# Attention with key pages as 64 rows of 4 KB in alternate lanes, sample queries and keys loaded by head in the projection, and 16 page places filled ahead

## The chip, the cores and the metric

The kernel runs on one core of a Trainium2 chip. The metric is the device time of one execution in microseconds, as the median of several runs; lower is better. Engines are called TensorE (PE in the profile; PEld is its weight load), VectorE (DVE), ScalarE (ACT), GpSimd (POOL) and SyncE (SP). SyncE issues nearly all DMAs here, in one order.

## The reference, cut to what matters

One step of a decoder layer: a prompt of 1024 new tokens, and 8 sequences with 8 new tokens each and 2048 cached ones in pages of 128. Everything is float32. Each of the two head groups has 512 columns of queries, keys and values.

```python
qd, kd, vd, qs, ks_, vs = project(rms_norm(x), w_in)          # 4 heads of 2*64, 8 heads of 64
past_d = cache_kv_diff[page_table]; past_s = cache_kv_sb[page_table]      # samples only
# group A: differential attention with a bias by distance
s = einsum('bqhcd,bkhcd->bchqk', q, k) * 64**-0.5 + bias      # c: two halves of 64
p = softmax(where(k_pos <= q_pos, s, -inf)); w = p[:, 0] - lam * p[:, 1]
o = rms_norm(einsum('bhqk,bkhe->bqhe', w, v)) * subln_g * (1 - lam_init)
# group B: stick-breaking attention, strictly causal
z = einsum('bqhd,bkhd->bhqk', q, k) * 64**-0.5
a = exp(log_sigmoid(z) + suffix_sum(log_sigmoid(-z)))         # 0 where k_pos >= q_pos
o = einsum('bhqk,bkhd->bqhd', a, v)
x = x + concat(oA, oB) @ w_out;  x = x + hmoe(rms_norm(x));  y = rms_norm(x)
```

The outputs are y and the new keys and values, for prompt and samples.

## The kernel before

**Stages.** `project`, `attention` of the differential kind, `attention` of the stick-breaking kind, `mix_out` (output projection), `route` and `experts` follow one another. Each stage is a block: an engine enters the next one when all engines have ended theirs.

**Projection.** Six groups of columns (keys, queries, values of each kind) by nine tiles of tokens, the ninth being the 64 sample tokens. Keys, and the queries of the sample tile, are turned by TensorE into `kT_ps`, copied by `keep_turned` (L391) and stored by SyncE's `store_turned` (L242) into `scratch_kT` and `scratch_qT`. In the last group SyncE also issues the first 14 places of cache pages (`AHEAD_PAGES`, L690), two places before each step; they lie where the first weight buffers were.

**Pages.** A page of keys is stored in memory turned, as 128 rows (two heads of 64) by four blocks of 128 keys, and a page of values as 128 tokens by 512 columns: 128 rows of 2 KB each. `load_page` (L920) fills one of 20 places with the pages of a pair of sequences, 256 KB each. In attention SyncE follows the order of TensorE's steps; after each step that used a place it waits for that step and issues the pages that come next into that place. A place holds both sequences side by side.

**Attention.** Four turns for each kind. A turn handles one block of two prompt heads (scores, softmax or stick-breaking, output) and one pair of sequences of the samples. The order of steps on each engine is written out by hand, one letter a step (`ORDERS`, L764). The sample's steps in one turn:
- `spread` (L1396) writes the pair's queries into `q_by_block`, which is zero elsewhere, so that one product gives the scores of two heads. In the first differential turn it first copies the loaded `sample_qT` into `sample_q_by_head`, in sixteen copies.
- `page_scores` (L1232): for two pages, eight products of 128x32 weights with 128x256 keys. 32 lanes of the result hold two blocks of one sequence; the 128 lanes are ordered by sequence, head, query.
- `peak`, `weigh` and `share` make the weights, `turn` turns them page by page, and one engine copies eight pages of `turns_and_scores_ps` to `sample_weights_T` (ScalarE L1607 for even groups, VectorE L1472 for odd ones).
- `apply` (L1273) multiplies four slices of 32 weight columns with the page's values into `sample_o_ps`, page after page.
- `rows` (L1475): in the differential kind three one-column operations (sum, inverse, factor), then the scaled copy `sample_o_rows`; `heads` (L1294) brings each head's part out with eight small products.

**The start of an attention stage.** In the differential kind SyncE waits for the projection's stores, then issues `sample_qT` (L1138), the first head's queries, keys, bias and values (L1093 to L1101), the places 14 to 19, `new_keys_T` (L1142) and the new values. At the end of a stage SyncE's last steps are the stores of head outputs (L1132) and loads of new values (L936).

## Time and profile before

| | before |
|---|---|
| Median of 3 runs | 1252.16 us (1251.69 to 1252.54) |
| The profiled execution | 1254.4 us, span 1252.6 us |
| Busy: TensorE, VectorE, ScalarE, GpSimd | 92%, 58%, 47%, 11% |
| DMA | 306.37 MB in 155135 packets, mean 245 GB/s |
| Projection, attention, output projection on, about | 0 to 323, 323 to 750, 750 to the end (us) |

Times are microseconds from the start of the span of one profiled execution. Busy times of an engine are summed over its instructions; matmuls are pipelined, so a busy TensorE isn't TensorE at its peak. The DMA share is the mean busy share of 16 DMA engines; overlapping packets let it go somewhat over 1. A granted clock of 1.00 is the full TensorE clock. "Issue" as the end of a wait is time in which the engine waited for nothing that the profile shows.

### The profile page before, as it was taken

How to read it: one execution, taken by the hardware profiler on the slowest of the kernel's cores; microseconds unless marked ns; L12 is line 12 of the kernel's file. 1: busy time of each engine (PE TensorE's matmuls, PEld its weight loads, DVE VectorE, ACT ScalarE, POOL GpSimd, SP SyncE). 2: the span in 40 equal slices, each digit the busy share in tenths (PEclk: the TensorE clock that was granted, in tenths of full speed). 3: DMA queues.
4: the chain of work that ended last, by engine and by line, in shares of the span. 5: the costliest groups of instructions: out<-in, count | busy, mean ns of one | idle time of the engine just before them, and what ended most of it. 6: DMA issues, size and time to landing. Idle time of an engine off the chain costs nothing. (4 is left out here: it accounts for less than half of the span.)

```text
span 1252.6 us, 23126 instructions
## 1 busy us (share of the span) xinstructions
PE 1146.3 (92%) x7593; PEld 797.8 (64%) x7593; DVE 723.5 (58%) x1078; ACT 591.9 (47%) x1015; POOL 138.8 (11%) x163
## 2 busy tenths in 40 slices
PE   7999999999689999969999999997599999999992
PEld 5877788778345555534655567875366666677771
DVE  6732112220367776568898977453566666666664
ACT  6520212101276776637568554232265555566644
POOL 0100000000011111100000000000123223333311
PEclk9999999999799999979999999999699999999997
DMA  7532424218699899999999935442689999764476
GB/s 265 197 107 70 141 97 127 75 53 277 216 380 382 305 382 380 377 374 381 386 380 382 364 113 187 155 147 103 250 312 365 370 373 302 212 182 102 103 218 193
DMA packets 155135, 306.37 MB, mean 245 GB/s; under 512 B 24359, under 2 KB 49354, under 8 KB 150922
## 3 DMA queue, kind: packets, MB, share of 16 engines
q1 hardware_dynamic: 144762, 271.33, 59.8%
q0 software_dynamic: 9216, 33.56, 11.2%
q8 instruction: 63, 1.03, 0.3%
q14 instruction: 54, 0.44, 0.1%
q10 hardware_dynamic: 1040, 0.00, 0.0%
HBM read 308.31 MB, written 53.67 MB: 289 GB/s over the span
## 5 line engine op out<-in xcount | busy, mean ns | idle before, releaser
L339 PE MATMUL proj_ps<-w_in_split,x_T_hi 128*128 128x512 f32 x608 | 188.9, 399 | 9.2 <-DVE w_in_split L387 9.2
L2566 DVE TENSOR_TENSOR w_gate_up_split<-w_gate_up,w_gate_up_split 128x2048 fp32r<-128x2048 f32 x62 | 139.3, 2288 | 84.3 <-ACT w_gate_up_split L2624 84.3
L2517 PE MATMUL gate_up_ps<-w_gate_up_split,slot_rows_T 128*128 128x512 f32 x744 | 177.7, 394 | 3.2 <-DVE slot_rows_T L2574 3.2
L2517 PEld LDWEIGHTS gate_up_ps<-w_gate_up_split,slot_rows_T 128*128 128x128 f32 x744 | 137.3, 188 | 32.2 <-DVE slot_rows_T L2574 4.4
L339 PEld LDWEIGHTS proj_ps<-w_in_split,x_T_hi 128*128 128x128 f32 x608 | 114.7, 189 | 36.7 <-issue 9.2
L503 ACT ACTIVATE proj_rows<-proj_ps,mean_squares 128x512 f32<-128x512 f32 x32 | 22.0, 688 | 213.6 <-PE proj_ps L339 188.6
L2624 ACT ACTIVATE w_gate_up_split<-w_gate_up 128x2048 fp32r x62 | 115.3, 1912 | 4.9 <-DMA w_gate_up<-in_w_up 3.1
L2539 PE MATMUL expert_out_ps<-w_down,expert_act_T 128*128 x256 | 115.3, 593 | 0.9 <-ACT expert_act_T L2647 0.9
L1192 PE MATMUL turns_and_scores_ps<-head_kT,head_qT 64*128 64x512 f32 (+3 forms) x384 | 86.5, 541 | 20.2 <-DMA head_kT<-scratch_kT 11.2
L339 PE MATMUL proj_ps<-w_in_split,x_T_lo 128*128 128x512 f32 x256 | 101.7, 397 | 0.0
L1786 PE MATMUL mix_out_ps<-w_out_split,oT_split 128*128 128x512 f32 x420 | 101.2, 396 | 0.3 <-DVE w_out_split L1925 0.3
L1786 PEld LDWEIGHTS mix_out_ps<-w_out_split,oT_split 128*128 128x128 f32 x420 | 77.6, 188 | 18.9 <-DVE w_out_split L1925 1.8
L1367 DVE TENSOR_TENSOR_SCAN rest_products<-rest_products 128x128 f32<-128x128 f32 (+7 forms) x64 | 84.3, 1344 | 3.4 <-ACT rest_products L1528 3.4
L333 PE MATMUL proj_ps<-x_T_hi,w_in_split 128*128 128x512 f32 x256 | 83.7, 402 | 0.0
L1556 ACT ACTIVATE weights_T<-turns_and_scores_ps 128x1024 f32<-128x1024 f32 (+6 forms) x80 | 58.9, 742 | 42.6 <-PE turns_and_scores_ps L1206 42.2
L2539 PEld LDWEIGHTS expert_out_ps<-w_down,expert_act_T 128*128 128x128 f32 x256 | 46.2, 190 | 47.1 <-issue 47.1
L2473 POOL DMA_INDIRECT scratch_x<-expert_out,slot_out x32 | 54.8, 1712 | 176.5 <-ACT expert_out L2655 82.3
L1290 PE MATMUL sample_o_ps<-pages,sample_weights_T 128*32 128x256 f32 x1024 | 71.1, 385 | 0.4 <-ACT sample_weights_T L1607 0.4
L1256 PE MATMUL turns_and_scores_ps<-pages,q_by_block 128*32 128x256 f32 x912 | 62.9, 400 | 5.1 <-ACT betas L1532 3.4
L387 DVE SCALAR_TENSOR_TENSOR w_in_split<-w_in_now,g_mix_T,w_in_split 128x512 fp32r<-128x512 f32 x48 | 35.6, 747 | 45.3 <-ACT w_in_split L491 45.3
L1192 PEld LDWEIGHTS turns_and_scores_ps<-head_kT,head_qT 64*128 64x128 f32 x384 | 30.8, 191 | 47.8 <-issue 26.4
L333 PEld LDWEIGHTS proj_ps<-x_T_hi,w_in_split 128*128 128x128 f32 x256 | 48.1, 188 | 14.4 <-DVE qk_transposed L421 2.7
(260 smaller groups left out, 1740.9 us busy)
## 6 DMA issues: line engine op xcount, KB each, us to landing
w_gate_up<-in_w_gate SPq DMA_DIRECT2D x34, 1024.0 KB, 8.5
w_gate_up<-in_w_up SPq DMA_DIRECT2D x34, 1024.0 KB, 10.4
w_down<-in_w_down SPq DMA_DIRECT2D x34, 1024.0 KB, 12.5
pages<-in_cache_v_d SPq DMA_DIRECT2D x128, 256.0 KB, 5.5
pages<-in_cache_kT_s SPq DMA_DIRECT2D x128, 256.0 KB, 5.4
pages<-in_cache_v_s SPq DMA_DIRECT2D x128, 256.0 KB, 5.8
pages<-in_cache_kT_d SPq DMA_DIRECT2D x100, 256.0 KB, 5.9
w_in_now<-in_w_in SPq DMA_DIRECT2D x48, 256.0 KB, 3.6
```

The source lines that it names most:

```text
L333: last = pe.matmul(pj_ps[:, n % PJ_BANKS, 0:c1 - c0], w[g % 2][:, k, at], h[:, k, c0:c1], start=(k == 0 and m == 0), stop=(k == KC - 1 and ...
L339: last = pe.matmul(pj_ps[:, n % PJ_BANKS, :], h[:, k, at], w[g % 2][:, k, :], start=(k == 0 and m == 0), stop=(k == KC - 1 and m == len(pa ...
L1192: last = pe.matmul(ring[places["score", it, i, g]][:, u, 0:k1 - k0], qT[half(u), it % 2, i * P:(i + 1) * P], kT[half(u), it % 2, k0:k1], s ...
L1256: last = pe.matmul(out, q_block[:, e, b, :], keys, start=(part == 0), stop=(part == 1))
L1290: last = pe.matmul(sO_ps[rows, :], sT[0:n, s, rows], page_v[0:n, c // 2, b:b + 2, :], start=(s == 0), stop=(s == D_PAGES - 1))
L1367: dve.tensor_tensor_scan(x, x, x, 1.0, ALU.mult, ALU.bypass).then_inc(scans.sem, 1)
L1556: act.activation(wT[:, at:at + m, :], blocks_of("out", it, i, n)[:, 0:m, :], ACT.Copy)\
L1786: last = pe.matmul(y_ps[:, m % Y_BANKS, :], oT_split[:, n % 2, a, k, :], w_split[:, b, k, c * BANK:(c + 1) * BANK], start=(m > 0 and at == ...
L2517: last = pe.matmul(gu_ps[:, u, :], xT[:, u, a, k, :], gu_split[:, u, b, k, :], start=(k == 0 and m == 0), stop=(k == KC - 1 and m == 2))
L2539: last = pe.matmul(y_ps[:, c, :], aT[:, u, k, :], w_dn[:, bass.ds(at, 1), k, c * BANK:(c + 1) * BANK] .rearrange("p a n -> p (a n)"), star ...
L2566: dve.tensor_tensor(gu_split[:, u, 1, at, :].rearrange("p k (c n) -> p k c n", c=2), raw[:, at, :, :], gu_split[:, u, 0, at, :].bitcast(F3 ...
L2624: act.activation(gu_split[:, u, 0, at, :].rearrange("p k (c n) -> p k c n", c=2), raw[:, at, :, :], ACT.Copy).then_inc(gu_hi.sem, 1)
```

## The change

1. The key cache is handed over with each page as 64 rows (the position in a head) by 8 heads by 128 keys: rows of 4 KB. `load_page` writes the keys of sequence e of a pair into lanes e, e+2, e+4, ... Value pages stay.
2. `q_by_head` holds a pair's queries head by head: lane 2d+e, columns 16u+8e to 16u+8e+7 of head h = 2c+u, zero elsewhere. The four times two products of `page_scores` take the same columns, and the lanes of the result are ordered by head, sequence, query.
3. Where the order by sequence is wanted again (`apply`), the evacuation of the turned weights permutes the columns, in two operations, one per sequence. The factors of the differential rows are computed in `weigh` and brought into that order by one product with a permuted identity (`rows_by_pair`) at the last `apply`.
4. The sample's turned keys and queries are stored by pair member (`scratch_sample_kT`, `scratch_sample_qT`) and loaded by head into alternate lanes in the projection's SyncE order (`load_by_head`, 16 DMAs). The loads of `sample_qT` and `new_keys_T` at the start of attention go, and the sixteen copies and a memset.
5. `AHEAD_PAGES` is 16 instead of 14. VectorE's differential order is edited: the second and third `weigh` of a turn (ww) stand behind its second `turn` (u).

```diff
@@ project
+        by_head_after = {(2, 3): (0, "k"), (3, 3): (0, "q"), (4, 3): (1, "k"), (5, 2): (1, "q")}
@@ store_turned
+                    if tile == PT:
+                        sp.dma_start((t.sample_kT if role == "k" else t.sample_qT_rows)[:, kind * 4:kind * 4 + 4, :, :],
+                                     qkT[:, n % 3, 0:4 * N_SAMPLE].rearrange("p (b e n) -> p b e n", b=4, e=PAIR))\
+                          .then_inc(qkT_stored[n % 3], 16)
+                        return
...
+                def load_by_head(kind, role):
+                    stored = staged[[s for s in turned if s[1] == PT and GROUPS[s[0]] == (kind, role)][0]]
+                    sp.wait_ge(qkT_stored[stored % 3], 16 * (stored // 3) + 16)
+                    src, dst = (t.sample_kT, t.new_kT) if role == "k" else (t.sample_qT_rows, t.sample_qT)
+                    for e in range(PAIR):
+                        for u in range(2):
+                            sp.dma_start(dst[e::PAIR, kind * KIND_HEADS + u:(kind + 1) * KIND_HEADS:2, :, :]
+                                         .rearrange("p b i n -> p b (i n)"),
+                                         src[HEAD * u:HEAD * u + HEAD, kind * KIND_BLOCKS:(kind + 1) * KIND_BLOCKS, e, :])\
+                              .then_inc(by_head_loaded, 16)
...
                     for n, step in enumerate(of_group[g]):
+                        if (g, n) in by_head_after:
+                            load_by_head(*by_head_after[g, n])
...
-        dve.memset(self.t.q_heads[:, :, :, :, :], 0.0).then_inc(self.zeroed, 1)
-AHEAD_PAGES = 14
+AHEAD_PAGES = 16
@@ load_page
-        sp.dma_start(t.page_rows[:, place, e, :, :], src[bass.ds(page, 1), :, :].rearrange("a k n -> (a k) n"))\
-          .then_inc(t.page_loaded[place], 16)
+        if name == "keys":
+            dst = t.page_rows[e::PAIR, place, :, :, :].rearrange("p e b n -> p (e b n)")
+        else:
+            dst = t.page_rows[:, place, e, :, :].rearrange("p b n -> p (b n)")
+        sp.dma_start(dst, src[bass.ds(page, 1), :, :].rearrange("a k n -> (a k) n")).then_inc(t.page_loaded[place], 16)
@@ attention, SyncE
-                    sp.dma_start(q_in[:, :, :], t.qT[:, :, SEQ:SEQ + N_SAMPLE]).then_inc(q_in_loaded, 16)
                     load_head(0)
...
-                    sp.dma_start(t.new_kT[:, :, :], t.kT[:, :, SEQ:SEQ + N_SAMPLE]).then_inc(t.new_kT_loaded, 16)
@@ attention, TensorE: page_scores and apply
                         for c in range(P // COL_TILE):
-                            e, b = c // 2, 2 * (c % 2) + part
+                            h, rows = 2 * c + part, slice(COL_TILE * c, COL_TILE * (c + 1))
...
-                                keys = pages[:, :, e, b, :]
-                            last = pe.matmul(out, q_block[:, e, b, :], keys, start=(part == 0), stop=(part == 1))
+                                keys = pages[:, :, h, :]
+                            last = pe.matmul(out, q_block[:, h, :], keys, start=(part == 0), stop=(part == 1))
...
+                    if kind == DIFF and s == D_PAGES - 1:
+                        pe.wait_ge(zeroed, 1 + PAIR)
+                        pe.wait_ge(sinv.sem, sinv.after(it, 2))
+                        last = pe.matmul(sO_ps[:, 2 * P:2 * P + 1], pair_first[:, :], sstat[:, 3:4], start=True, stop=True)
@@ attention, VectorE: spread, weigh, turn, rows
-                    for odd in range(2):
-                        dve.tensor_copy(q_block[:, :, odd::2, 16 * odd:16 * odd + 16],
-                                        t.q_heads[:, it * PAIR:(it + 1) * PAIR,
-                                                  KIND_BLOCKS * kind + odd:KIND_BLOCKS * (kind + 1):2, :, :]
-                                        .rearrange("p s b u q -> p s b (u q)")).then_inc(q_spread.sem, 1)
+                    for e in range(PAIR):
+                        for u in range(2):
+                            col = 2 * DEC_SEQ * u + DEC_SEQ * e
+                            dve.tensor_scalar_mul(q_block[:, u::2, col:col + DEC_SEQ],
+                                            t.sample_qT[:, KIND_HEADS * kind + u:KIND_HEADS * (kind + 1):2, it, :], t.pair_map[:, e:e + 1])\
+                               .then_inc(q_spread.sem, 1)
...
+                    elif n == 2:
+                        dve.wait_ge(sweighed.sem, sweighed.after(it, 1))
+                        dve.wait_ge(applied.sem, applied.after(it, -1))
+                        dve.tensor_tensor(sstat[:, 5:6], sstat[:, 1:2], sstat[:, 4:5], ALU.add).then_inc(sinv.sem, 1)
...
+                        dve.tensor_tensor(sstat[:, 3:4], sstat[:, 2:3], t.row_factor[:, :], ALU.mult)\
+                           .then_inc(sinv.sem, 1)
...
-                        dve.tensor_copy(sT[:, pages[0]:pages[-1] + 1, :], blocks_of("turn", it, g)[:, 0:len(pages), :])\
-                           .then_inc(read("turn", it, g), 1)
+                        cols = blocks_of("turn", it, g)[:, 0:len(pages), :]
+                        dve.tensor_copy(by_pair(sT[:, pages[0]:pages[-1] + 1, :], 0), of_pair(cols, 0))
+                        dve.tensor_copy(by_pair(sT[:, pages[0]:pages[-1] + 1, :], 1), of_pair(cols, 1)).then_inc(read("turn", it, g), 1)
...
-                        dve.tensor_scalar_mul(o_rows_s[:, :], sO_ps[:, :], sstat[:, 3:4]).then_inc(rows_kept.sem, 1)
+                        dve.tensor_copy(sstat[:, 6:7], sO_ps[:, 2 * P:2 * P + 1]).then_inc(sinv.sem, 1)
+                        dve.wait_ge(sinv.sem, sinv.after(it, 3))
+                        dve.tensor_scalar_mul(o_rows_s[:, :], sO_ps[:, 0:2 * P], sstat[:, 6:7]).then_inc(rows_kept.sem, 1)
@@ attention, ScalarE: turn
+                        act.activation(by_pair(sT[0:n, pages[0]:pages[-1] + 1, :], 0), of_pair(cols, 0), ACT.Copy)
+                        act.activation(by_pair(sT[0:n, pages[0]:pages[-1] + 1, :], 1), of_pair(cols, 1), ACT.Copy)\
+                           .then_inc(read("turn", it, g), 1)
@@ host
-        cache = cache.reshape(n_pool, PAGE, 2, KIND_BLOCKS, P)
-        host["cache_kT_" + name] = cache[:, :, 0].transpose(0, 3, 2, 1).reshape(n_pool, P, HALF_W)
+        cache = cache.reshape(n_pool, PAGE, 2, KIND_HEADS, HEAD)
+        host["cache_kT_" + name] = cache[:, :, 0].transpose(0, 3, 2, 1).reshape(n_pool, HEAD, KIND_HEADS * PAGE)
```

The lane map of `halves` follows the new lane order, and `spread` of the near bias takes its head from the new order too.

## Rows read from the trace of the kernel before

**Rows 1.** Stretches: start:end length, busy us (instructions) per engine, granted clock, DMA share, GB/s

```profile
200.00:300.00 100.00, 100.00 (x442) 80.18 (x441) 20.97 (x31) 12.63 (x21) 0.00 (x0) 1.00 0.36 120
440.00:535.00 95.00, 88.04 (x941) 53.15 (x933) 61.61 (x138) 61.34 (x145) 12.53 (x29) 1.00 1.04 380
535.00:720.00 185.00, 167.86 (x1924) 99.77 (x1926) 158.02 (x213) 115.82 (x204) 0.00 (x0) 0.95 1.04 378
```

**Rows 2.** Waits of TensorE from 331 to 751 us: total us, times, longest

```profile
PE turns_and_scores_ps L1192 <- DMA head_kT<-scratch_kT: 11.2, 1, 11.2
PE turns_and_scores_ps L1192 <- issue: 5.3, 1, 5.3
```

**Rows 3.** SyncE's queue in order of time: start, us, operation, count

```profile
497.83 17.20 SPq L927 DMA_DIRECT2D pages<-in_cache_v_d  x22
...
522.09 12.47 SPq L927 DMA_DIRECT2D pages<-in_cache_kT_s  x18
534.98 0.80 SPq L1132 DMA_DIRECT2D scratch_oT<-head_oT  x2
535.97 1.99 SPq L936 DMA_DIRECT2D new_values<-out_new_kvs  x2
```

**Rows 4.** Order of time around the end of the differential stage, with idle time before

```profile
529.64 1.50 PE L1290 MATMUL sample_o_ps<-pages,sample_weights_T 128*32 128x256 f32 x24
...
533.07 0.60 DVE L1393 TENSOR_SCALAR head_oT<-turns_and_scores_ps,sub_g 128x128 f32<-128x128 f32 x2
...
533.21 1.08 PE L1299 MATMUL sample_o_ps<-ident,sample_o_rows 128*128 128x32 f32 x8 [1.19 <-DVE sample_o_rows L1488]
...
539.63 1.66 PE L1192 MATMUL turns_and_scores_ps<-head_kT,head_qT 64*128 64x128 f32 x8 [5.35 <-issue]
```

**Rows 5.** DMA, 378 to 390 us: packets by size; queue: packets, MB, share

```profile
DMA packets 2541, 4.63 MB, mean 386 GB/s; under 512 B 280, under 2 KB 280, under 8 KB 2541
...
q1 hardware_dynamic: 2541, 4.63, 104.8%
```

**Rows 6.** DMA from 731 to 736 us

```profile
DMA packets 436, 1.55 MB, mean 311 GB/s; under 512 B 57, under 2 KB 57, under 8 KB 436
...
q1 hardware_dynamic: 436, 1.55, 78.3%
```

**Rows 7.** DMA issues from 440 to 535 us: count, KB each, median us to landing

```profile
pages<-in_cache_kT_d SPq DMA_DIRECT2D x32, 256.0 KB, 5.4
pages<-in_cache_kT_s SPq DMA_DIRECT2D x26, 256.0 KB, 5.1
```

**Rows 8.** Stretches of lower clock, columns as in rows 1

```profile
323.50:337.20 13.70, 5.66 (x42) 2.25 (x42) 4.96 (x26) 1.15 (x5) 0.00 (x0) 0.50 0.88 290
535.20:548.80 13.60, 7.56 (x62) 3.65 (x62) 5.71 (x18) 3.72 (x9) 0.00 (x0) 0.50 0.97 357
```

**Rows 9.** SyncE's queue at the start of attention

```profile
324.35 0.61 SPq L1138 DMA_DIRECT2D sample_qT<-scratch_qT  x1
```

**Rows 10.** TensorE's first scores

```profile
331.54 0.80 PE L1192 MATMUL turns_and_scores_ps<-head_kT,head_qT 64*128 64x128 f32 x4 [11.22 <-DMA head_kT<-scratch_kT]
```

**Rows 11.** SyncE's waits from 0 to 320 us

```profile
SPq L239 <- ACT proj_rows L503: 79.4, 25, 5.2
```

**Rows 12.** Operations that are split (min/median/max ns), one of 128x512 (busy, mean ns)

```profile
L1607 ACT ACTIVATE sample_weights_T<-turns_and_scores_ps x16: 250/634/1047, 359.2 to 724.0; 128x1024 f32<-128x1024 f32 x8, 8x128 f32<-8x128 f32 x8
L1472 DVE COPY sample_weights_T<-turns_and_scores_ps x8: 1202/1218/1225, 381.8 to 723.0; 128x1024 f32<-128x1024 f32 x8
...
L1412 DVE COPY q_by_block<-sample_q_by_head x16: 171/189/197, 329.5 to 657.7; 128x64 f32<-128x64 f32 x16
...
L1336 DVE TENSOR_TENSOR scores<-turns_and_scores_ps,near_bias 128x512 f32<-128x512 f32 x24 | 16.5, 686 | 13.0 <-PE turns_and_scores_ps L1192 6.8 <-ACT scores L1521 5.9 <-issue 0.3
```

**Rows 13.** DMA from 321 to 324.3 us: the store of 64 lanes

```profile
DMA packets 80, 0.13 MB, mean 40 GB/s; under 512 B 16, under 2 KB 16, under 8 KB 80
...
q1 hardware_dynamic: 80, 0.13, 17.2%
```

More of the change, by code:

```diff
@@ L555, in keep @@
         return ctx.enter_context(nc.sbuf_tensor(name, shape, dt))
-    t.q_heads = keep("sample_q_by_head", [P, DEC_BATCH, BLOCKS, 2, DEC_SEQ])
+    t.sample_qT = keep("sample_q_by_head", [P, 2 * KIND_HEADS, TURNS, DEC_SEQ])
+    t.new_kT = keep("new_keys_by_head", [P, 2 * KIND_HEADS, TURNS, DEC_SEQ])
     t.near_dec = keep("near_bias_sample", [P, 2, PAGE + DEC_SEQ])
@@ L561, in table_places @@
     t.sub_g = keep("sub_g", [P, 1])
+    t.pair_map = keep("map_of_pair", [P, PAIR])
     t.pages = keep("page_ids", [1, DEC_BATCH * N_PAGES], I32)
@@ L614, in spread @@
             rows = slice(DEC_SEQ * n, DEC_SEQ * (n + 1))
-            for kind, head in ((DIFF, n // 2 % H_DIFF), (STICK, H_DIFF)):
+            for kind, head in ((DIFF, n // PAIR // 2), (STICK, H_DIFF)):
                 sp.dma_start(t.near_dec[rows, kind, :], distances(t, head, DEC_SEQ, PAGE + DEC_SEQ))\
@@ L683 @@
 KIND_BLOCKS = BLOCKS // 2
+KIND_HEADS = 2 * KIND_BLOCKS
 COL_TILE = 32
@@ L1046, in attention @@
         sT_done = count("sample_weights_T_in_psum", V_GROUPS)
-        q_in = sb("sample_qT", [P, BLOCKS, N_SAMPLE if kind == DIFF else 1])
-        q_in_loaded = sem("sample_qT_loaded")
         zeroed = sem("constants_written")
-        q_spread = count("q_by_block_done", 2)
+        q_spread = count("q_by_head_done", 2 * PAIR)
         ps_done = count("page_scores_in_psum", S_GROUPS)
@@ L1054, in attention @@
             speaks = count("sample_peaks_done", S_GROUPS)
-            sinv = count("sample_inverse_sums", 3)
+            sinv = count("sample_inverse_sums", 4)
         else:
@@ L1234, in page_scores @@
                     if g == 0:
-                        pe.wait_ge(q_spread.sem, q_spread.after(it, 1))
+                        pe.wait_ge(q_spread.sem, q_spread.after(it, 2 * PAIR - 1))
                     new = not pages_of_step(kind, ("page_scores", it, g))
-                    if new:
-                        pe.wait_ge(t.new_kT_loaded, 16)
-                    else:
-                        pages = pages_here(pe, "page_scores", it, g)
+                    if not new:
+                        pages = pages_here(pe, "page_scores", it, g).rearrange("p a e b n -> p a (e b) n")
                     place_free(pe, "page_scores", it, g)
@@ L1397, in spread @@
                     if it == 0:
-                        dve.memset(q_block[:, :, :, :], 0.0).then_inc(zeroed, 1)
+                        dve.memset(q_block[:, :, :], 0.0).then_inc(zeroed, 1)
                         if kind == DIFF:
-                            dve.wait_ge(q_in_loaded, 16)
-                            for u in range(2):
-                                for s in range(DEC_BATCH):
-                                    dve.tensor_copy(t.q_heads[half(u), s, :, u, :], q_in[half(u), :, DEC_SEQ * s:DEC_SEQ * (s + 1)])\
-                                       .then_inc(zeroed, 1)
-                            dve.wait_ge(zeroed, 1 + 2 * DEC_BATCH)
+                            for e in range(PAIR):
+                                dve.tensor_copy(by_pair(pair_first[:, :].unsqueeze(1), e), of_pair(t.ident[:, :].unsqueeze(1), e))\
+                                   .then_inc(zeroed, 1)
+                            dve.wait_ge(zeroed, 1 + PAIR)
                         else:
@@ L1410, in spread @@
                     dve.wait_ge(ps_done.sem, ps_done.after(it, -1))
-                    for odd in range(2):
-                        dve.tensor_copy(q_block[:, :, odd::2, 16 * odd:16 * odd + 16],
-                                        t.q_heads[:, it * PAIR:(it + 1) * PAIR,
-                                                  KIND_BLOCKS * kind + odd:KIND_BLOCKS * (kind + 1):2, :, :]
-                                        .rearrange("p s b u q -> p s b (u q)")).then_inc(q_spread.sem, 1)
+                    for e in range(PAIR):
+                        for u in range(2):
[3 more added lines that the diff above has]
+                               .then_inc(q_spread.sem, 1)
                 def page_scores(it, g):
@@ L1606, in turn @@
                         act.wait_ge(applied.sem, applied.after(it, pages[-1] - D_PAGES))
-                        act.activation(sT[0:n, pages[0]:pages[-1] + 1, :], blocks_of("turn", it, g)[0:n, 0:len(pages), :],
-                                       ACT.Copy).then_inc(read("turn", it, g), 1)
+                        cols = blocks_of("turn", it, g)[0:n, 0:len(pages), :]
+                        act.activation(by_pair(sT[0:n, pages[0]:pages[-1] + 1, :], 0), of_pair(cols, 0), ACT.Copy)
+                        act.activation(by_pair(sT[0:n, pages[0]:pages[-1] + 1, :], 1), of_pair(cols, 1), ACT.Copy)\
+                           .then_inc(read("turn", it, g), 1)
                 steps = dict(score=score, out=out, page_scores=page_scores, turn=turn)
@@ L2712, in host_constants @@
     mask_rows[1, H_DIFF] = 1
-    half = np.arange(P) // DEC_SEQ % 2
+    half = np.arange(P) // (PAIR * DEC_SEQ) % 2
+    pair_of_lane = np.tile(np.eye(PAIR, dtype=np.float32), (P // PAIR, 1))
     half_map = np.stack([1 - half, half], 1).astype(np.float32)
```

71 lines of the change are left out of this document (38 added, 33 removed).

## The prediction

> **What bounds the kernel now.** I read the stages first (busy time and DMA share per stretch), then the waits of TensorE, then SyncE's queue, since the change is about transfers. In the projection TensorE is busy 100 of 100 us and the DMA share is 0.36. In attention TensorE is busy 88.04 of 95 us and 167.86 of 185 us, while the DMA share stands at 1.04: both look full [rows 1]. TensorE's waits decide which one is the bound. The two long ones lie at the edges of the attention stages: 11.2 us for the first head's keys, and 5.3 us between the differential and the stick-breaking stage [rows 2]. Behind these the list goes on with waits of about 1 us for VectorE and ScalarE, and names no page. So pages come early enough. As a check: the last page DMAs of differential values leave SyncE until 515.03 [rows 3]; with the median landing of 5.1 to 5.4 us that page DMAs have there [rows 7] they are there at about 520, and TensorE's last use of a page in that stage runs until 531.1 [rows 4]: some 10 us of cover. A faster page is worth nothing on the page itself.
>
> It is worth something where SyncE, late behind a full DMA system, holds up the end of a stage. SyncE issues pages until 534.56, then two stores of head outputs, then two small loads of new values that take 1.99 us because the queue is full, and is through at 537.96 [rows 3]. TensorE was through at about 534.3; the next stage's first product comes at 539.63 [rows 4]. Those are the 5.3 us.
>
> **The change part by part.**
>
> *Key pages as 64 rows of 4 KB.* First the price of a packet by its size; completions (4 bytes, the count under 512 B) are taken as nothing. From 378 to 390 us nearly only pages move: 104.8% of 16 engines over 12 us is 201.2 us for 2541 - 280 = 2261 packets of 2 KB, 89.0 ns each [rows 5]. From 731 to 736 only output weights in rows of 4 KB move: 78.3% x 16 x 5 = 62.6 us for 436 - 57 = 379 packets, 165 ns each [rows 6]. A key page costs 128 x 89.0 / 16 = 712 ns of DMA time now and 64 x 165 / 16 = 661 ns after the change, 51 ns less. 32 + 26 = 58 key pages are issued between 440 and 535 us [rows 7], a stretch in which SyncE has no wait for another engine, so its lateness adds up: 58 x 51 ns = 3.0 us less of it at the end. SyncE can't be done before the last head output is evacuated at 533.67 [rows 4] plus one store and the two small loads, about 534.8, so at most 3.1 us can be had. I take 3.0: the next stage starts at about 536.6. But there TensorE runs at a granted clock of 0.50, the lower of its two levels (1.2 GHz), busy 7.56 of the 9.2 us from 539.6 to 548.8 [rows 8]. If that stretch ends when it did, the time won is worth 3.0 x (1 - 0.5 x 0.82) = 1.8 us. Bounds: 0 (packets of 4 KB into every second lane are no faster; slower is rival 1) and 3.1. In the stick-breaking stage the same saving meets no wait: nothing.
>
> *Sample queries and keys by head, loaded in the projection.* Out of the start of attention go a load of 256 KB ahead of the head's queries and keys, issued at 324.35 for 0.61 us [rows 9], one like it behind them, and sixteen 64x64 copies on VectorE, which were done before the first scores at 331.54 [rows 10]. SyncE reaches the head's loads 0.65 us sooner, and 1024 packets of 256 B (128 lanes by 8 blocks) are gone: by bytes of the 2 KB packet 1024 x 11 / 16 = 0.7 us, and up to twice that. I take 1.15 us, bounds 0.65 and 2.0. TensorE then restarts inside a stretch at 0.50 clock that it fills (5.66 us of work from 331.54 to 337.2) [rows 8], so half counts: 0.6. In the projection sixteen loads of 256 packets, one constant's load and the page loads of the next part are put into SyncE's order. What they are moved past are stores of rows and the next weights; SyncE waits there 79.4 us for evacuated rows alone [rows 11], row buffers are reused three steps later, and the added waits are for stores made several steps before. Cost 0. Without that cover, four issues of about 0.45 us would hold up the stores behind them by 2 us a group. The memset taken from VectorE's start lay in the 9 us before the first product: 0.
>
> *16 places ahead.* Four page loads move from about 327 us into the idle DMA share of the projection. SyncE catches up with TensorE sooner, and it catches up before 440 us anyhow: 0.
>
> *A pair's sequences in every second lane.* The page products keep their number and shape (eight, 32 columns of weights against 256 of keys). What is added:
> - The sample weights' evacuation is split in two by sequence. On ScalarE it takes up to 1047 ns for 128x1024 and 250 ns for 8x128; by these two the fixed part is about 140 ns, so 16 evacuations cost 2.2 us more. On VectorE 1218 ns become two of 128x512, whose nearest row has 686 ns: 8 x 0.15 = 1.2 us [rows 12].
> - The spread of queries goes from two copies of 189 ns [rows 12] to four operations on 128x32 of 0.16 to 0.19 us (estimate: a little under the 128x64 copy): 8 x 0.33 = 2.6 us on VectorE.
> - The differential turn's three one-column statistics move ahead of the last page, where they wait for ScalarE's second exponential, which the evacuation ahead of them in the queue has already needed. From the last page to the rows two of three steps go, about 0.35 us; SyncE is later than that anyway: 0.
> - TensorE gets one product per differential turn that brings the factors into the rows' order: one of the four pairs of records that took 1.08 us [rows 4], 0.27 us, 1.1 us in all, of which I count 0.8, since it shortens waits behind it. Bounds 0 and 1.1.
>
> Of the 6.0 us on ScalarE and VectorE TensorE sees what its other work doesn't cover. Queued behind these operations are scores, which TensorE waits for through its three PSUM places. It is busy 91 to 93% of the time [rows 1], and its waits name many operations in small parts, so I take an eighth, 0.7 us; bounds 0 and 6.0.
>
> **Sum.** -0.6 - 1.8 + 0.8 + 0.7 = -0.9 us. The profiled execution took 1254.4 us, 1.8 of it around its span of 1252.6; the runs shown have a median of 1252.16. Carried over to it: 1251.3 us, less than a measurement of this kernel can tell from no change (0.2%, 2.5 us). With the nearer bounds of the parts the forecast's own range is 1248.5 to 1255.
>
> **Rivals.**
> 1. *Shared parts of the lanes (slower).* Only one transfer of before has 16 engines serve 64 lanes: the store at 323 us took 17.2% x 16 x 3.3 = 9.1 us for 64 packets of 2 KB, 142 ns each [rows 13], against 89.0 over 128 lanes. Engines that meet in one part of the lanes slow one another by 1.6. If the rows of a page in every second lane are dealt out so that engines meet, a key page costs up to 64 x 284 / 16 = 1.14 us, 0.42 more. It decides from the first nanoseconds beyond today's 712: 58 x 0.05 us would turn the gain at the stage's end into a loss of 2.9. At the full price 58 x 0.42 = 24 us exceed the 10 us of cover, TensorE waits for pages, and over 96 + 128 keys in attention it comes to 94 us less some 15 of cover: 1330 us; at half price about 1275. For it: that row. Against it: all parts of the lanes are reached, and value pages in 128 lanes lie between.
> 2. *No fall of the clock (faster).* If the shorter gap spares the stretch at 0.50, its 7.56 us of products become 3.8, and the 3.0 us count in full: -0.9 - 3.8 - 1.2 = -5.9, 1246.3. For it: the gap is more than halved. Against it: the stretch at 0.50 begins by 535.2 [rows 8], within 1 us of the last product.
> 3. *The rows are no faster.* If memory and not the packet sets 380 GB/s, the end of the stage stays and +0.9 remains: 1253.1. Against it: in full share the pages moved 4.63 MB in 12.6 us, 368 GB/s [rows 5], the 4 KB rows 1.55 MB in 3.9, 396 [rows 6].
>
> The Trainium skill, "SBUF — State Buffer", in its section on the DMA port swizzle, has a transfer's rate go by how many of 16 ports its lanes reach, 8 of them for lanes 0 to 63; the store of 64 lanes agrees (142 against 89.0 ns). By that rule alone every second lane of 128 reaches all 16, and rival 1 would not happen. The Trainium skill's "DMA: Bandwidth & Descriptors", in its section on the descriptor swizzle, gives each engine a port of its own for 128 lanes. Dealt by rows, four in turn per engine, a page in every second lane would put each engine on two ports that it shares with another, and the time would be rival 1's. No row of before shows which of the two holds here.
>
> **How the numbers follow.** Forecast 0.50 (0.10 faster, 0.36 same, 0.04 slower); rival 2 0.24, faster; rival 1 0.22, slower; rival 3 0.04, same. Faster 0.34, same 0.40, slower 0.26. The range reaches down to rival 2's 1246 and up into rival 1's mild part, 1262; beyond lie less than 2 in 10, most of it rival 1 at its dearer prices.
>
> **What would show it.** Right: TensorE's gap before the stick-breaking stage near 2.3 us with a stretch at 0.50 behind it; first scores at about 330.4; packets of 4 KB near 165 ns in a stretch of pages; the halves of the evacuation near 0.6 us on ScalarE and 0.69 on VectorE; no wait for pages. Wrong: key pages that land well after 5.4 us or fewer GB/s in attention (rival 1), a granted clock of 1.00 after the gap (rival 2), the gap unchanged (rival 3), or ScalarE's and VectorE's part in TensorE's waits grown by over 2 us.

## The result: 0.75% slower

| | before | after |
|---|---|---|
| median, us | 1251.93 (1251.44 to 1252.54, 4 runs) | 1261.19 (1260.41 to 1264.14, 4 runs) |
| profiled execution, us (span) | 1254.4 (1252.6) | 1261.38 (1259.5) |

The ratio is 1.0075, 95% interval 1.006 to 1.0089. The range 1246 to 1262 held the time; the forecast of no clear change was wrong. The two traces are 6.9 us apart in their spans, the medians 9.3: the profiled execution of the kernel before (1254.4) was slower than the four of its median, so lines before and after show somewhat less than the whole difference.

The same stretches of the kernel after, columns as in [rows 1]. The projection is as full as it was, but the DMA engines of the attention stages no longer are (share 0.99 against 1.04, 354 against 380 GB/s), and TensorE does 1.4 us less work in the first of the two stretches in attention and 5.5 us less in the second:

```profile
200.00:300.00 100.00, 100.00 (x442) 80.14 (x442) 21.15 (x33) 12.61 (x21) 0.00 (x0) 1.00 0.35 114
440.00:535.00 95.00, 86.66 (x925) 52.58 (x921) 61.05 (x139) 59.78 (x144) 12.95 (x28) 0.99 0.99 354
535.00:720.00 185.00, 162.36 (x1876) 94.86 (x1876) 154.13 (x216) 112.24 (x203) 0.00 (x0) 0.94 0.99 354
```

TensorE's long waits in the kernel after (total us, times, longest). The wait for the first head is 2.1 us shorter than in [rows 2]; the one between the two attention stages, called the gap below, is 7.6 us longer:

```profile
PE turns_and_scores_ps L1231 <- issue: 12.9, 1, 12.9
PE turns_and_scores_ps L1231 <- DMA head_kT<-scratch_kT: 9.1, 1, 9.1
```

SyncE's queue of the kernel after (start, us, operation, count). The 18 page DMAs that took 12.47 us in [rows 3] take 14.59, and it is through at 543.23 instead of 537.96:

```profile
525.40 14.59 SPq L960 DMA_DIRECT2D pages<-in_cache_kT_s  x18
540.42 0.83 SPq L1173 DMA_DIRECT2D scratch_oT<-head_oT  x2
541.44 1.79 SPq L968 DMA_DIRECT2D new_values<-out_new_kvs  x2
```

TensorE around the end of the differential stage in the kernel after, beside [rows 4]. Its last product of the stage comes 2.3 us sooner (530.93 against 533.21), the first of the next one 5.3 us later:

```profile
530.93 1.08 PE L1337 MATMUL sample_o_ps<-ident,sample_o_rows 128*128 128x32 f32 x8 [0.77 <-DVE sample_o_rows L1528]
544.90 1.65 PE L1231 MATMUL turns_and_scores_ps<-head_kT,head_qT 64*128 64x128 f32 x8 [12.89 <-issue]
```

One DMA instruction for a page, on SyncE, from 440 to 535 us (min/median/max ns, first and last start), first in the kernel before, then in the kernel after. These rows explain the rest. The instruction for a value page takes SyncE 333 ns in both (the median); the one for a key page takes 333 ns in 128 rows of 2 KB and 475 ns in 64 rows of 4 KB, and its shortest time (332 against 474) says the same, so it is not a wait in a full queue:

```profile
L927 SPq DMA_DIRECT2D pages<-in_cache_v_d x69: 332/333/2703, 439.8 to 514.7; - x69
...
L927 SPq DMA_DIRECT2D pages<-in_cache_kT_d x32: 332/333/1292, 442.8 to 486.7; - x32
...
L927 SPq DMA_DIRECT2D pages<-in_cache_kT_s x26: 332/333/893, 515.5 to 534.2; - x26
```

```profile
L960 SPq DMA_DIRECT2D pages<-in_cache_v_d x65: 332/333/2584, 439.7 to 516.2; - x65
...
L960 SPq DMA_DIRECT2D pages<-in_cache_kT_d x32: 474/475/607, 440.6 to 487.9; - x32
...
L960 SPq DMA_DIRECT2D pages<-in_cache_kT_s x20: 474/475/783, 518.0 to 534.7; - x20
```

The forecast on the packets held nevertheless, where the engines have enough to do. From 443 to 451 us they still have a backlog, since ten value pages went out just ahead of the key pages, and the kernel after moves more than the one before (403 against 386 GB/s, both at a full share; its packets of 4 KB take 164 ns in the mean there, forecast 165). From 525.5 to 539.9 us key pages alone have been issued for some time, and SyncE can't fill the engines (0.84, 288 GB/s, where the kernel before has 1.04 and 377 from 522.2 to 534.5 us). Before, then after:

```profile
443.00:451.00 8.00, 7.74 (x115) 4.18 (x112) 6.24 (x11) 5.53 (x13) 1.09 (x2) 1.00 1.05 386
522.20:534.50 12.30, 10.46 (x124) 6.27 (x116) 5.01 (x17) 2.79 (x9) 1.90 (x4) 1.00 1.04 377
```

```profile
443.00:451.00 8.00, 7.59 (x112) 4.66 (x105) 5.73 (x12) 5.34 (x16) 1.57 (x4) 1.00 1.03 403
525.50:539.90 14.40, 5.74 (x63) 3.56 (x62) 1.74 (x6) 0.77 (x3) 0.74 (x2) 0.75 0.84 288
```

SyncE's lateness goes on growing behind the gap. The last page DMAs of attention, and the first product of mix_out, before and then after: SyncE is through with its last cache page at 727.1 instead of 712.7 us, and mix_out starts 6.4 us later, nearly all of the 6.9 us between the spans. But 5.3 of the 6.4 us stand already at the first product behind the gap (544.90 against 539.63); of the rest of SyncE's lateness TensorE sees 1.1 us:

```profile
694.88 17.81 SPq L927 DMA_DIRECT2D pages<-in_cache_v_s  x24
```

```profile
751.13 3.67 PE L1776 MATMUL mix_out_ps<-pages,oT_tiles 128*128 128x512 f32 x8 [0.80 <-PEq L1069]
```

```profile
711.36 15.70 SPq L960 DMA_DIRECT2D pages<-in_cache_v_s  x24
```

```profile
757.57 3.67 PE L1818 MATMUL mix_out_ps<-pages,oT_tiles 128*128 128x512 f32 x8 [0.80 <-PEq L1110]
```

### The profile page after: what moved, and what is told of

Same layout as the page of the kernel before. It is cut to its first block and busy times, and to the rows that moved or that the text cites. A ratio compares the mean times of both kernels' runs of the same rounds, so it can differ in the third digit from the quotient of the medians.

```text
span 1259.5 us, 23192 instructions
## 1 busy us (share of the span) xinstructions
PE 1150.0 (91%) x7601; PEld 800.6 (64%) x7601; DVE 725.3 (58%) x1095; ACT 592.6 (47%) x1031; POOL 142.6 (11%) x163
## 3 DMA queue, kind: packets, MB, share of 16 engines
q0 software_dynamic: 9216, 33.56, 11.3%
## 5 line engine op out<-in xcount | busy, mean ns | idle before, releaser
L1231 PE MATMUL turns_and_scores_ps<-head_kT,head_qT 64*128 64x512 f32 (+3 forms) x384 | 86.2, 539 | 25.3 <-issue 12.9
L2515 POOL DMA_INDIRECT scratch_x<-expert_out,slot_out x32 | 57.7, 1803 | 180.1 <-DMA scratch_x<-expert_out,slot_out 95.9
L1290 PE MATMUL turns_and_scores_ps<-pages,q_by_head 128*32 128x256 f32 x896 | 61.8, 400 | 4.6 <-ACT betas L1572 3.0
L1207 POOL TENSOR_SCALAR stats<-stats 128x1 f32<-128x1 f32 x32 | 9.5, 297 | 433.0 <-ACT o_squares L1606 433.0
```

The lines of the kernel that those rows point to most:

```text
L1231: last = pe.matmul(ring[places["score", it, i, g]][:, u, 0:k1 - k0], qT[half(u), it % 2, i * P:(i + 1) * P], kT[half(u), it % 2, k0:k1], s ...
L1290: last = pe.matmul(out, q_block[:, h, :], keys, start=(part == 0), stop=(part == 1))
```

## The experiments

Three theories. **A, issue**: the key page's DMA instruction takes SyncE 475 instead of 333 ns, and SyncE becomes the pace. **B, packets**: the 64-row transfers load the lanes or the engines more. **C, the rest**: loads in the projection, 16 ahead, split evacuation, factor product. Every ratio is to the kernel before on the same chip, with its 95% interval. The chips are not all the same: beside runs 1 to 4 the kernel before has a median of 1251.23 us, beside 5 to 8 one of 1253.84, beside 9 to 12 one of 1254.67. No trace of it was kept from there, so times in microseconds are compared within these groups, and positions against the one trace of the kernel before only with care. "Mix_out starts" is its first product.

**1. After, key pages by 128 rows** (same bytes; the keys come to stand in a wrong order, so only the time is read).

```diff
+        rows = src[bass.ds(page, 1), :, :].rearrange("a k (u n) -> (a k u) n", u=2)
+        dst = t.page_rows[:, place, e, :, :].rearrange("p b n -> p (b n)")
```

> The changed kernel with one part undone: each key page is again moved by 128 rows of 2 KB into 128 lanes (the same bytes of memory, so the keys stand in the wrong order in the place; only the time is read). Theory A (issue): a DMA of 64 rows costs SyncE 475 ns instead of 333 ns, so SyncE falls further behind and ends the differential stage late; undoing the form brings the gap before the stick-breaking stage from 12.9 back to about 5 to 6 us, the two us won at the start of attention stay, and the time is 1250 us. Theory B (lanes): packets into every second lane are slow; the same time, but packet rate and not issue would have to explain it. Theory C (the rest): the split evacuations, the spread of queries and the added product are what costs; the time stays at 1261.

1251.87 us, ratio 0.9999 (0.9985 to 1.0012), gap 4.6 us. The whole loss goes with the form of the key transfer, and C costs nothing that the time shows. A and B are not yet told apart. SyncE's queue in this run, to be held against the 14.59 us above:

```profile
518.92 12.32 SPq L960 DMA_DIRECT2D pages<-in_cache_kT_s  x18
531.67 0.81 SPq L1173 DMA_DIRECT2D scratch_oT<-head_oT  x2
532.66 1.78 SPq L968 DMA_DIRECT2D new_values<-out_new_kvs  x2
```

**2 and 3. Before, key pages by 64 rows**, into every second lane, and into 64 neighbouring lanes (the edit is shortened; the keys' order is again wrong).

```diff
+        if name == "keys":
+            dst = t.page_rows[e::PAIR, place, :, :, :]               # run 2
+            dst = t.page_rows[HEAD * e:HEAD * e + HEAD, place, ...]  # run 3
```

> The kernel before with one part of the change alone: each key page moved by 64 rows of 4 KB into every second lane (the keys' order in the place is not the one that the products expect; only the time is read). Theories A and B: about 1260 to 1262, the gap between the attention stages from 5.3 to about 12 us; A adds that in a stretch of key pages alone SyncE needs about 0.8 us a page with the DMA share below 0.9. Theory C: 1252.

> The kernel before with each key page moved by 64 rows of 4 KB into 64 neighbouring lanes, sequence 0 of a pair into lanes 0 to 63 and sequence 1 into 64 to 127 (order of the keys as in the one with alternate lanes wrong; only the time is read). If the issue cost hangs on the number of rows, a key page's DMA takes SyncE 475 ns here too; if it hangs on the step between lanes, 333. If the part of the lanes that a transfer reaches sets its rate, packets of 4 KB take up to 284 ns (twice the 142 ns of a 2 KB packet in the store of 64 lanes) and the kernel is far slower, 1300 us or more; if lanes don't matter, it is as fast as the one with alternate lanes, about 1260.

Run 2: 1264.38 us, 1.0101 (1.0076 to 1.0125), gap 12.1 us, so this one part done alone brings the whole loss. Run 3: 1392.54 us, 1.113 (1.11 to 1.116). A stretch in which key and value pages are issued, in run 2, then run 3, columns as in [rows 1]: both have full engines, but neighbouring lanes move 276 GB/s and alternate lanes 388. From 440 to 535 us a packet of 4 KB has a median of 266 ns in run 3, 159 in run 2.

```profile
444.00:455.80 11.80, 11.40 (x146) 6.21 (x138) 8.27 (x17) 8.90 (x22) 1.83 (x4) 1.00 1.02 388
```

```profile
444.00:455.80 11.80, 8.87 (x83) 4.51 (x75) 3.12 (x7) 5.22 (x16) 0.74 (x2) 0.86 1.04 276
```

TensorE's waits in run 3 from 331 to 900 us name pages, as neither kernel's list does in its upper lines; and yet one key DMA costs SyncE 469 ns there, the same as in alternate lanes (475). The two costs are separate: the issue goes with the form, the rate with the lanes. Run 3 alone is held up by its packets.

```profile
PE turns_and_scores_ps L1259 <- DMA pages<-in_cache_kT_d: 21.2, 7, 4.2
PE turns_and_scores_ps L1259 <- DMA pages<-in_cache_kT_s: 15.8, 5, 4.3
PE sample_o_ps L1293 <- DMA pages<-in_cache_v_s: 14.0, 8, 2.7
```

```profile
L931 SPq DMA_DIRECT2D pages<-in_cache_kT_d x40: 468/469/1266, 442.6 to 527.4; - x40
```

**4. Before, its own transfers, with work added on SyncE**: two semaphore increments behind each key page (`own_wait` is such an increment).

```diff
+        if name == "keys":
+            for _ in range(2):
+                own_wait(sp, t)
```

> The kernel before with two semaphore increments (about 60 ns each) added to SyncE's queue after each key page, and the old transfers. Theory A: SyncE's time per page is what makes it late, so 0.12 us more for each of the 58 key pages between 440 and 535 us is up to 7 us more lateness, less what the full DMA queue had made it wait anyway: the gap grows from 5.3 to 8 to 12 us and the time is 1255 to 1259. Theory B, and any in which the DMA engines set the pace before: the added work hides behind the queue's waits, 1252.

1261.14 us, 1.008 (1.0056 to 1.0103), gap 10.7 us; the time expected by A was 1255 to 1259, so the effect was under-sized. Its DMAs are those of the kernel before (128 rows); only time on SyncE was added, and a loss as large as the change's is there. The 18 page DMAs take 14.91 instead of 12.47 us, 0.136 us more each where about 0.12 was expected to be added: none of it hid behind the DMA engines. A is shown, B isn't needed. SyncE's queue:

```profile
524.49 14.91 SPq L927 DMA_DIRECT2D pages<-in_cache_kT_s  x18
539.92 0.81 SPq L1135 DMA_DIRECT2D scratch_oT<-head_oT  x2
540.91 2.06 SPq L939 DMA_DIRECT2D new_values<-out_new_kvs  x2
```

**5. After, 12 page loads left for the next stage.**

```diff
-LATE_PAGES = 7
+LATE_PAGES = 12
```

> The changed kernel, with 12 instead of 7 page loads of the crossing left for after the start of the stick stage. Everything is computed as in the changed kernel. Each load is two DMAs (one for each sequence of the pair), so SyncE has 10 DMAs less before the end of the first stage, at 0.81 us each (18 in 14.59 us in the trace of after) 8.1 us. Theory A (SyncE's time for a page sets the end of the stage): SyncE reaches the store of oT at about 532 instead of 540.4 us, TensorE's gap there falls from 12.9 to about 5 us, and the time from 1261.2 to about 1253 (1251 to 1255). Theory B (the loads are only moved: the 12 pages are wanted soon in the stick stage, whose DMA engines are full, so they come late there): the gap falls, but waits for pages of 4 to 8 us stand in 545 to 620 us, and the time stays at 1258 to 1262. Theory C (the rest of the change): no gap change matters, 1261.

1265.81 us, 1.009 (1.0072 to 1.0107). A, as it stood, fell here: the gap closed (12.9 to 3.5 us) and nothing was won. It came as this run's theory B had it, that the moved pages come late afterwards. TensorE's waits from 535 to 757 us in this run:

```profile
PE turns_and_scores_ps L1290 <- DMA pages<-in_cache_kT_s: 6.1, 3, 2.7
...
PE turns_and_scores_ps L1231 <- issue: 3.5, 1, 3.5
```

Waits for value pages add 1.1 us. SyncE's last cache page leaves at 730.65 us, 3.6 us later than in the kernel after. So SyncE isn't late for one deadline; it is the pace of the whole stretch from 440 us to its last page. Its records bear it out: counting the idle stretches over 0.25 us between them, the kernel before has 11.3 us of them from 340 to 440, 3.8 from 440 to 660 and 4.0 from 660 us to its last page at 712.7, and rests for 13.3 us soon behind that; the kernel after has 7.9 and 2.8 us, and 0.7 from 660 to 720, still issuing pages. The kernel before was thus near the same state, and just kept up. Moving loads can't help an engine that hardly rests. Runs 7 and 9 test that.

**6. Before, 10 page loads left.**

```diff
-LATE_PAGES = 7
+LATE_PAGES = 10
```

> The kernel before, with 10 instead of 7 page loads left for after the start of the stick stage: 6 DMAs at 0.69 us less on SyncE before the end of the stage, 4.2 us. Theory A: SyncE was 3.6 us late even in the kernel before (it ended at 537.96, TensorE's last product at 534.3), so the gap of 5.35 us falls to 2.5 to 3.5 us and the time to 1248 to 1250, against 1251.2 of the kernel before. Theory B (moved loads come late afterwards): 1251 to 1253, with a page wait in 540 to 600 us. If what remains of the gap is the way of the last result through store and load, not SyncE's backlog: no change.

1253.68 us, 0.9997 (0.9985 to 1.0009). In the trace the gap is 2.6 us and mix_out starts at 746.81, 4.3 us sooner than in the trace of the kernel before. The time doesn't show it, and 1248 to 1250 was expected: a miss. In the two traces mix_out to the end of the span takes 503.9 instead of 501.5 us, and TensorE's granted clock stands at 0.50 for 30.7 instead of 27.3 us of it (the last stretch of the span left out); what that is worth is taken up below, under what is left open.

**7. After, page numbers fetched by 8.**

```diff
-IDS = 4
+IDS = 8
```

> The changed kernel, but SyncE fetches the page numbers 8 at a time instead of 4, so half as many loads of numbers from SBUF (some 300 ns each in the trace of after, one for 4 DMAs). Everything is computed as in the changed kernel. Theory A: SyncE gains about 37 ns a DMA, in the 100 us before the end of the stage 4 to 5 us; its 18 DMAs before the end take 13.9 instead of 14.6 us, TensorE's gap falls from 12.9 to 8 or 9 us, and the time to about 1257 (1255 to 1259). Theory B (DMA packets or lanes, not issue): nothing moves, 1261.

1260.78 us, 1.0064 (1.0047 to 1.0081). Less work on SyncE: the last page leaves at 723.4 (727.1), mix_out starts at 753.34 (757.57), 4.2 us sooner, as A in its new form has it, SyncE as the pace of the whole stretch. The gap is 10.8 us, where 8 or 9 was expected. The span is only 0.8 us shorter, with 37.5 us at 0.50 after mix_out instead of 34.1. Expected were 4 us in the time; the interval overlaps that of the kernel after (1.006 to 1.0089), so the time shows no gain that is clear of noise: a miss.

**8. Before, runs 6 and 7 together and the sample's queries loaded after the first head.**

> The kernel before with three moves on SyncE: 10 page loads left for the stick stage, page numbers 8 at a time, and the load of the sample's queries at the start of the attention behind the four of the first head. Theory A: the gap at the end of the first stage falls from 5.35 to 2.5 to 3.5 us, the wait for the first head's keys from 11.2 to about 10 us, the time to 1247 to 1249.5. Theory B (as in the run with the 10 late loads alone): 1250 to 1253.

1258.09 us, 1.0029 (1.0017 to 1.0042): a miss. First scores come 1.7 us sooner (329.8), but the first product with pages comes 3.4 us later (335.7 against 332.3), because the queries it needs are now behind four loads (it waits 5.1 us for `q_by_block`), and mix_out starts at 752.3.

**9 and 12. Page numbers fixed in the program**, in the kernel after and the kernel before (the page table is not followed; the edit is shortened).

```diff
-        page = t.page_ids.of(name, it * PAIR + e, page_at(kind, s))
+        page = ((it * PAIR + e) * N_PAGES + page_at(kind, s)) * 37 % (DEC_BATCH * N_PAGES)
```

> The changed kernel with page numbers fixed in the program (a fixed shuffle of the 128 pages in place of the page table), so SyncE has no load of page numbers and no address work; the DMAs, their rows, bytes and waits are the same. What it leaves out: the page table is not followed. Theory A (SyncE's time for a page is the pace from 440 us on: 352 page DMAs between 440 and 726.7 us, 0.81 us each, SyncE idle for 0.7 us in each of those stretches): a key DMA then costs SyncE about 0.53 us and a value DMA 0.39, so it waits again, its last page goes out before 712 us (726.7 in after), the gap at the end of the first stage falls from 12.9 to 3 to 5 us, mix_out starts before 749 us (757.6 in after) and the time is 1246 to 1251. Theory B (the 64-row packets or lanes are slow): the DMA engines remain the pace, 1258 to 1262.

> The kernel before with the same fixed page numbers (the page table is not followed). Beside the run of the changed kernel with fixed numbers it shows what 4 KB rows are worth when SyncE is not the pace. Theory A: SyncE in the kernel before was nearly the pace already (0.69 us a page and 17.3 us idle in 660 to 720), so the gap falls from 5.3 to about 3 us and mix_out starts at 747 to 750 instead of 751.1; time 1246 to 1251, and the changed kernel with fixed numbers is 1 to 3 us below this one, by its earlier start. Theory B: this one 1250 to 1252 and the changed kernel 8 us above it.

Run 9: 1253.23 us, 0.999 (0.9978 to 1.0002). Run 12: 1254.2 us, 0.9994 (0.998 to 1.0007). With the same 64-row key DMAs the loss is gone once SyncE has less to do between them: the 64-row transfers themselves are not slow. Both times miss the 1246 to 1251 that A expected, though mix_out starts before 749 us in both, and the two can't be told apart by time. Run 9, then run 12, columns as in [rows 1]: in the traces the 4 KB rows move more, 391 against 386 and 395 against 382 GB/s, and mix_out starts at 746.54 against 747.79.

```profile
440.00:500.00 60.00, 57.44 (x634) 33.58 (x631) 42.41 (x95) 41.16 (x103) 8.82 (x18) 1.00 1.04 391
545.00:660.00 115.00, 106.93 (x1287) 64.70 (x1287) 102.31 (x141) 72.79 (x135) 0.00 (x0) 1.00 1.04 395
```

```profile
440.00:500.00 60.00, 57.17 (x627) 33.40 (x623) 41.48 (x93) 41.34 (x103) 7.94 (x19) 1.00 1.05 386
545.00:660.00 115.00, 107.52 (x1262) 64.96 (x1261) 100.07 (x130) 73.15 (x131) 0.00 (x0) 0.99 1.05 382
```

SyncE of run 9 in the same stretch as the two kernels above. The medians rise from 475 to 596 ns and from 333 to 432, as I read it because the instruction now waits for room in full queues; the minima are the old prices, so the 64-row form is the dearer one with a fixed page number too. The pace is back with the DMA engines.

```profile
L960 SPq DMA_DIRECT2D pages<-in_cache_v_d x64: 327/432/6218, 446.2 to 506.4; - x64
...
L960 SPq DMA_DIRECT2D pages<-in_cache_kT_d x29: 472/596/1523, 440.0 to 480.7; - x29
```

**10. Before, runs 6 and 7's edits together.**

> The kernel before with 10 page loads left for the stick stage and page numbers fetched 8 at a time (the load of the sample's queries stays first). Theory A: as with the 10 late loads alone, a gap of about 2.6 us and mix_out at 746 to 747 us (751.1 in before); what is won up to there (4 to 5 us) is kept only if TensorE's clock does not stay at 0.50 longer in the routing and expert stages, where it stayed 27.3 us in before, 30.7 and 37.5 us in the last two versions of this. 1247 to 1252. Theory B (loads only moved): 1251 to 1253.

1253.73 us, 0.9996 (0.9983 to 1.0009), where 1247 to 1252 was expected; mix_out starts at 746.16, 5 us sooner than in the trace of the kernel before, and the rest takes 3.8 us longer than there. No version tried beats the kernel before.

**11. After, each 4 KB row in two pieces.**

```diff
+            rows = src[bass.ds(page, 1), :, :].rearrange("a k (u n) -> (a k) u n", u=2)
```

> The changed kernel with each 4 KB row of a key page written as two pieces of 2 KB in the same lane (64 lanes, two pieces), everything else the same and computed the same. If the DMA keeps the two pieces, this tells whether SyncE's 475 ns goes with 64 lanes or with the 4 KB rows: by the number of descriptors (128, as in the kernel before) the instruction falls to about 333 ns, SyncE is no longer the pace and the time is 1250 to 1253; by the number of lanes it stays at 475 ns and 1259 to 1263. If the two pieces are joined again on the way to the chip, the trace shows the same 64 elements of 4096 B and 1261.

1264.21 us, 1.0074 (1.0052 to 1.0096), a key DMA at 475 ns. Inconclusive: the pieces are one run of memory on both sides, the trace shows 64 elements of 4096 B as in the kernel after, and the price is that of this form. Whether 64 rows or 64 lanes make the instruction dear stays open.

## Why the prediction was wrong

**Bound now.** "SyncE, late behind a full DMA system, holds up the end of a stage" named the right engine and place and half the reason: I took its lateness for the DMA engines' alone. SyncE's own work per page, 0.69 us on 18 DMAs in [rows 3], was already as long as the engines needed (0.71 us by the prediction), and run 4 shows that work added to it lengthens the stage at once. The two small loads of new values, read as slow "because the queue is full" (1.99 us), take 1.79 us in the kernel after too, behind a stretch at a share of 0.84; a full queue alone doesn't explain them.

**Key pages as 64 rows: the step that failed.** Forecast was that 58 key pages, each 51 ns cheaper, would take 3.0 us off SyncE's lateness, bring the gap to near 2.3 us and start the next stage at 536.6. Measured: SyncE through 5.3 us later, the gap 12.9 us, the start at 544.90. The price of a packet was right where the engines are full: in run 9 from 545 to 660 us packets of 4 KB take 164 ns in the mean (forecast 165), and in run 12 those of 2 KB 88 (89.0 in the prediction); in the kernel after, with the engines no longer full, the median is 159 and the mean 178. The term was credited with 1.8 us and its bounds were 0 and 3.1, because only the transfer was priced, as if SyncE's pace were that of the DMA engines. The price of the instruction on SyncE was left out, which puts its growth at nothing without a reason, and the trace of before had a sign of it. Its 64-row store on SyncE, beside stores of the same line in 128 rows (ns as above):

```profile
L239 SPq DMA_DIRECT2D out_new_kvs<-proj_rows x4: 348/349/349, 300.6 to 317.4; - x4
```

```profile
L239 SPq DMA_DIRECT2D out_new_kvs<-proj_rows x1: 486/486/486, 322.0 to 322.0; - x1
```

I used that very store for rival 1's packets [rows 13] and not for its issue. Priced with the 475 ns that the kernel after shows: 18 key DMAs before the stage's end cost 18 x 142 ns = 2.6 us more there (14.59 - 12.47 = 2.1 measured), and 58 of them 8.2 us, where 3.0 of gain stood. Over the 160 key DMAs from 440 us on it is 22.7 us; 14.4 us of them are seen at SyncE's last page and 6.4 at mix_out. What covers the rest, idle time of SyncE or pages that come ahead of their use, wasn't separated.

**Sample loads in the projection.** Right in its direction and too small: the first scores were forecast 1.15 us sooner, at 330.4, and come 2.0 us sooner, at 329.52, the upper bound. The projection paid nothing (100 of 100 us busy, and its end within 0.1 us of before), although each by-head load costs SyncE some 617 ns, where 0.45 was assumed.

**16 ahead.** Forecast 0; run 1, which keeps it, stands at 0.9999, and no run tried it alone.

**Every second lane.** The evacuations came as sized: 128x512 at about 620 ns on ScalarE and 682 on VectorE (forecast 0.6 and 0.69). The factor product takes 0.38 us a turn, two overlapping records of 0.26 (forecast 0.27), and a spread operation 0.23 (forecast 0.16 to 0.19), so VectorE got more work than was counted. The price of 0.7 + 0.8 us on TensorE can't be seen: TensorE's listed waits for ScalarE and VectorE from 331 to 757 us add up to 26.1 us against 28.1 before, and run 1 stands at 0.9999, with an interval about as wide as this price.

**Rivals.** 1, shared lanes, gave the sign but not the cause: it forecast landings well over 5.4 us (the medians of key pages are 4.6 and 4.0 us from 440 to 535) and full engines at a lower rate, and neither came; run 3 shows that its mechanism exists for neighbouring lanes. That the range held the time is luck: its upper end, 1262, had been put there for this rival. By the rule that I cited from the Trainium skill's "SBUF — State Buffer", section on the DMA port swizzle, every second lane reaches all 16 ports: run 2's 388 GB/s agrees, and so does run 3's 276 for 64 neighbouring lanes. The reading with two engines to a port, which I worked out from the descriptor swizzle in the Trainium skill's "DMA: Bandwidth & Descriptors" (whose list is for 128 lanes only), did not show. 2, no fall of the clock: the change didn't test it, since the gap grew, and the stretch at 0.50 with it, from 13.7 to 20.5 us. Runs 6, 8, 9, 10 and 12 did: their gap is 2.6 us, and the clock still stood at 0.50 for 10.2 us around it, so the rival fell. 3, rows no faster, fell by the traces of runs 9 and 12 (395 against 382 GB/s at the same share).

**What is left open.** Run 1 starts mix_out 3.3 us sooner than the kernel before and its span is 3.6 us shorter, while the medians are equal. Runs 6 and 10 have a lead of 4.3 and 5.0 us at mix_out and no gain in the time. It is tempting to say that TensorE's clock took the lead back, since they stand at 0.50 for longer behind it, but the traces don't show that. From mix_out on the program is the same in all kernels, and that part takes 501.3 to 506.0 us in the fourteen traces, with 27.3 to 37.5 us at 0.50 (the last stretch of the span left out). It is longest, 506.0, in run 11, which has no lead at all, and its length goes rather with the chip: 501.3 to 504.1 in runs 1 to 4, 503.9 to 505.8 in runs 5 to 8, 504.6 to 506.0 in runs 9 to 12, and the medians of the kernel before on these chips rise likewise. With no trace of the kernel before from there, it isn't known where its mix_out starts beside these runs, and whether the leads exist stays open.

## What to carry to other kernels

Price a DMA twice: its bytes on the engines and its instruction on the engine that issues it, and compare both per page with the time between pages. When an issuing queue shows almost no idle time, it is a bound like any other: moving its work about won nothing here (run 5), less work per transfer took the loss away (run 9). Before a lead at one stage is called won or lost later, trace both kernels on the same chip. Look in the trace for the new shape's instruction in any transfer, however unlike, before calling its issue unchanged.

## Unexpected about the hardware

- Half the rows, at twice the size, made the DMA instruction longer on SyncE: 475 and 469 ns (64 rows of 4096 B, alternate and neighbouring lanes) against 333 (128 rows of 2048 B); one store of 64 rows of 2048 B took 486, those of 128 rows 349.
- Alternate lanes and neighbouring lanes differ by far: 388 against 276 GB/s at a full share, from 444 to 455.8 us in runs 2 and 3.
- The same program from mix_out on took 501.3 to 506.0 us in fourteen traces from several chips, 27.3 to 37.5 us of it at a granted clock of 0.50. Differences of a few microseconds ahead of it can't be followed to the end from one trace each.
